# A three-slot weight ring placed at other distances from the activations, in a TensorE-bound decoder kernel

## The reference

```python
def swiglu(h, w_gate, w_up, w_down):
    return (jax.nn.silu(h @ w_gate) * (h @ w_up)) @ w_down

for l in range(DEPTH):                                   # DEPTH = 2
    x = x + 0.5 * swiglu(rms_norm(x, ffn1_norm[l]), ...)  # 1024 -> 2816 -> 1024
    h = rms_norm(x, mix_norm[l])
    pa, pb, pc, pd = jnp.split(h @ w_in[l], IN_SPLITS, axis=-1)
    ...                                                   # four attention mixers
    x = x + jnp.concatenate([ya, yb, yc, yd], axis=-1) @ w_out[l]
    x = x + 0.5 * swiglu(rms_norm(x, ffn2_norm[l]), ...)
    x = rms_norm(x, final_norm[l])
# then one layer of the second kind, with w_in_2 of 1024 x 7424
```

## Time and profile before

| | us |
|---|---|
| median of 2 runs | 1314.11 (1311.85 to 1316.36) |
| the profiled execution | 1319.89 |
| its span, first to last instruction | 1317.6 |
| PE busy | 1265.6 (96%) |
| weight loads busy | 1239.5 (94%) |
| DVE busy | 841.5 (64%) |
| ACT busy | 640.0 (49%) |

### The profile page before, as it was taken

One profiled execution on the slowest core, in us unless ns is written; L12 is line 12 of the kernel. 1 busy time (PEld: TensorE's weight loads), 2 busy tenths in 40 slices (PEclk: granted clock), 3 DMA queues, 4 the chain that ended last, 5 costly groups with the idle time before them and its releaser, 6 DMA issues.

```text
span 1317.6 us, 24755 instructions
## 1 busy us (share of the span) xinstructions
PE 1265.6 (96%) x10500; PEld 1239.5 (94%) x10500; DVE 841.5 (64%) x1059; ACT 640.0 (49%) x850; POOL 78.7 (6%) x57
## 2 busy tenths in 40 slices
PE   6999999988999999999999997999999999999997
PEld 6999999978999999999999996899999989899995
DVE  5766677775676666876667686476666754446665
ACT  4433346754543334533335764453333554766542
POOL 1110011210000000000000211000000000000000
PEclk9999999986999999999999995799999999999999
DMA  8876665320565655566665530256655655415542
GB/s 287 219 227 206 191 224 172 114 87 2 182 200 193 191 191 192 170 199 195 194 219 163 166 132 12 65 165 219 192 191 191 200 178 174 128 58 168 176 152 105
DMA packets 169514, 220.33 MB, mean 167 GB/s; under 512 B 5280, under 2 KB 152480, under 8 KB 169312
## 3 DMA queue, kind: packets, MB, share of 16 engines
q1 hardware_dynamic: 165680, 213.66, 50.8%
q0 software_dynamic: 2080, 2.48, 1.0%
q10 hardware_dynamic: 1680, 3.13, 0.7%
HBM read 218.15 MB, written 3.42 MB: 168 GB/s over the span
## 4 chain that ended last, share of the span: by engine, by line
PE 86%; ACT 6%; DVE 5%; issue 1%; DMA 1%; SPq 0%; POOLq 0%; POOL 0%; DVEq 0%; ACTq 0%
PE pj L433 12%; PE pj L437 12%; PE pj L436 12%; PE acc L437 8%; PE acc L436 8%; PE acc L433 8%; PE tr L433 6%; PE tr L437 6%; PE tr L436 6%; PE acc L616 4%; ACT probs L994 2%; ACT w_hi L875 1%; PE tr L608 1%; DVE w_lo L1186 1%; PE tr L586 1%
## 5 line engine op out<-in xcount | busy, mean ns | idle before, releaser
L1186 DVE TENSOR_TENSOR w_lo<-raw,w_hi 128x2048 fp32r<-128x2048 f32 (+2 forms) x206 | 459.4, 2230 | 241.7 <-ACT w_hi L875 240.3
L875 ACT ACTIVATE w_hi<-raw 128x2048 fp32r<-128x2048 f32 (+2 forms) x206 | 381.2, 1854 | 395.3 <-PE pj L433 142.0
L433 PE MATMUL pj<-hT_hi,w_hi 128*128 128x256 f32 x992 | 277.2, 279 | 3.0 <-DVE w_lo L1186 2.4
L437 PE MATMUL pj<-hT_hi,w_lo 128*128 128x256 f32 x992 | 275.8, 278 | 0.0
L436 PE MATMUL pj<-hT_lo,w_hi 128*128 128x256 f32 x992 | 275.7, 278 | 0.0
L437 PE MATMUL acc<-act_hi,w_lo 128*128 128x256 f32 x704 | 194.3, 276 | 0.0
L433 PE MATMUL acc<-act_hi,w_hi 128*128 128x256 f32 x704 | 194.3, 276 | 0.0
L436 PE MATMUL acc<-act_lo,w_hi 128*128 128x256 f32 x704 | 194.3, 276 | 0.0
L433 PEld LDWEIGHTS pj<-hT_hi,w_hi 128*128 128x128 f32 x992 | 187.5, 189 | 4.5 <-DVE w_lo L1186 2.6
L436 PEld LDWEIGHTS pj<-hT_lo,w_hi 128*128 128x128 f32 x992 | 187.3, 189 | 0.0
L437 PEld LDWEIGHTS pj<-hT_hi,w_lo 128*128 128x128 f32 x992 | 187.1, 189 | 0.0
(11 more groups left out here) (212 smaller groups left out, 1989.6 us busy)
## 6 DMA issues: line engine op xcount, KB each, us to landing
raw<-in_w_in SPq DMA_DIRECT2D x47, 1024.0 KB, 5.3
raw<-in_ffn_w_up SPq DMA_DIRECT2D x44, 1024.0 KB, 5.3
raw<-in_ffn_w_down SPq DMA_DIRECT2D x44, 1024.0 KB, 5.0
raw<-in_ffn_w_gate SPq DMA_DIRECT2D x43, 1024.0 KB, 5.4
raw<-in_w_out SPq DMA_DIRECT2D x12, 1024.0 KB, 4.9
raw<-in_w_proj_a SPq DMA_DIRECT2D x4, 512.0 KB, 3.5
raw<-in_w_proj_b SPq DMA_DIRECT2D x4, 512.0 KB, 3.9
raw<-in_w_proj_c SPq DMA_DIRECT2D x4, 512.0 KB, 3.4
```

The lines of the kernel that those rows point to most:

```text
L433: ins = pe.matmul(out, lhs[0], rhs[0], start=first, stop=False, **kw)
L437: return pe.matmul(out, lhs[1], rhs[0], start=False, stop=last, **kw)
L875: act.activation(w_hi[r % RING][:, 0:w], raw[r % RING][:, 0:w], ACT.Copy).then_inc(hi_set, 1)
L1186: dve.tensor_tensor(w_lo[r % RING][:, 0:w], raw[r % RING][:, 0:w], w_hi[r % RING][:, 0:w].bitcast(F32), ALU.subtract).then_inc(lo_set, 1)
```

## The change

The six tensors `w_hi0..2` and `w_lo0..2` become two, each with three rows of 2048 + 64 elements. A ring slot is a view into a row that starts 60, 4 or 44 elements behind the row's start.

```diff
-        w_hi = [sb(f"w_hi{i}", [P, SLOT], F32R) for i in range(RING)]
-        w_lo = [sb(f"w_lo{i}", [P, SLOT], F32R) for i in range(RING)]
+
+        shift = (60, 4, 44)
+        halves_hi = sb("w_hi", [P, RING, SLOT + 64], F32R)
+        halves_lo = sb("w_lo", [P, RING, SLOT + 64], F32R)
+        w_hi = [halves_hi[:, i, shift[i]:shift[i] + SLOT] for i in range(RING)]
+        w_lo = [halves_lo[:, i, shift[i]:shift[i] + SLOT] for i in range(RING)]
```

## The result

The changed kernel took 1350.88 us (1348.23 to 1353.54, two runs) against 1314.11 us before. The ratio is 1.028 with an interval of 1.0164 to 1.0395, so it is slower for certain, and whether by more than 2% this comparison leaves open. The two medians differ by 37 us, but each rests on two runs. The forecast was 1314 with a range that ended at 1342.

What follows compares the result with a forecast made beforehand. The prediction took PE's matmul rate as the bound. Its terms for instructions, splits and matmuls were all 0, giving 1319.9 + 0 for the profiled execution, or 1314 us for the median; own range 1306 to 1322, stretched to 1284 to 1342.

Steps and rivals of the forecast that it cites:

- Instructions, DMAs and splits: Whole kernel: no instruction or wait changes, DMA target stays put, and the splits L875 and L1186 keep their times; 0 us.
- The bound of a tenth: Splits L875 and L1186: upper bound on their slowdown from shifted starts, a tenth of their mean, 0.19 and 0.22 us.
- Two distances carry the same two rhythms, so the distance has little say: 256-column matmuls: distances +64 and -64 (192 modulo 256) both show 113.3 and about 117.5 ns between starts.
- the term of 0 us for the matmuls: About 9,260 ring-reading matmuls: slots keep their rhythm, loops stay short, mixers' mix is dealt anew; 0, plus or minus 5 us.
- The prediction's own sign of being wrong: Starts within gate, up and down slots: three different rhythms would prove the distance sets the rhythm by itself.
- the prediction's picture of two rhythms that are dealt anew at restarts: Mixer slots: the mix of short (113.3 ns) and long (about 117.5 ns) start spacing is redrawn at restarts; 0 us.
- the border at 185.55: End of a SwiGLU loop before the mixer: said to change the distance yet keep the short rhythm, 113.3 ns.
- The short rhythm is the moving operand's own limit: 256-column matmuls: 113.3 ns lies on the line through 384 and 512 columns, so no distance can beat it.
- the faster rival: 256-column matmuls: a rhythm below 113.3 ns, saving 26 us (1288) or 48 us (1266); chance 0.16.
- The rival that slots fall into the long rhythm: Ring slots turn long as the distance changes at slot borders: 8 us one, 24 all loops, 31 everything (1322 to 1345); 0.30.
- The rival that the change does nothing: Whole kernel: PE never waits for another engine and has two independent read ports, so time stays 1314; no separate chance.
- The small shifts of single starts: 160-column matmuls, whose distance changes per chunk: starts 0.10, 0.12, 0.11 us apart, shifting a few ns with the address.

Runs made afterwards that it cites:

- the kernel with 64 and 144: Kernel before, with ring views by direction: stationary minus moving stays 64 where weights are stationary, becomes 144 where they move; 1313.48 us against 1320.13, ratio 0.9959.

## Why the prediction was wrong

*Instructions, DMAs and splits: right.* Orders and counts are the same, and L1190 and L879 took 2225 and 1852 ns. The bound of a tenth was not needed.

*Two distances carry the same two rhythms, so the distance has little say: wrong, and this is the step that failed.* The reading of the stretch at 196.43 stands: a distance of 192 can carry the short rhythm. What failed is the inference from two distances to all others, and with it the term of 0 us for the matmuls. The three distances that the change brings can't carry it in the loops: their slots went from 113.3 ns to 117.9 at 48, 118.5 at 80 and 117.3 at 240, and 28 us of the loss are in the SwiGLU slots. The prediction's own sign of being wrong was three ring slots with three different rhythms, and it came.

*Nor are 64 and 192 equals.* With stationary weights all slots of the loops hold the short rhythm at 64, and at 192 they run at 117.9 throughout. With moving weights all eleven slots at 64 had it in one run and about three quarters in another, and at 192 only four of 29 in the kernel before. But 192 isn't closed to it either: the run with the gate slot alone entered it there behind a slot at 117.7, and one token-major slot of the kernel before took it up after an interruption of 4 us. These are its second and its last matmul:

```profile
1148.29 0.28 PE L436 MATMUL pj<-w_lo,hT_hi 128*128 128x256 f32 x1
...
1153.50 0.28 PE L437 MATMUL pj<-w_hi,hT_lo 128*128 128x256 f32 x1
```

5.21 us / 46 = 113.3 ns. In the run with shifts of 0, where this slot has the same distance, it ran at 117.8. So at 64 and 192, outside the loops, the prediction's picture of two rhythms that are dealt anew at restarts was right, with the odds depending on distance and direction. I sorted the stretches by what they showed and not by direction, and so took the two distances for equals.

*A misread border.* The prediction says that the border at 185.55 changed the distance and kept the rhythm. The slots on both sides of 185.55 have their weights stationary (`acc<-act_hi,w_hi`); the direction changes at 196.43. There the rhythm did hold, so the argument stands with the other time.

*The short rhythm is the moving operand's own limit: never beaten at 256 columns, but its argument is refuted.* Over 17 distances in either direction nothing with 256 columns came below 113.3 ns, and the faster rival, at 0.16, had no case. The argument was a line through 113.3, 173.3 and 233.3 ns for 256, 384 and 512 columns, and its last point is no limit. These are two starts, 24 matmuls apart, of the 512-column projection in the kernel with 64 and 144:

```profile
1288.94 0.39 PE L441 MATMUL acc<-w_hi,hT_hi 128*128 128x512 f32 x1
...
1294.38 0.39 PE L441 MATMUL acc<-w_hi,hT_hi 128*128 128x512 f32 x1
```

5.44 us / 24 = 226.7 ns, twice 113.3, in three of its four slots, and in one slot of the run with three multiples of 64, where the distance is 0. With 144 everywhere the same four slots took 231 to 232 ns. So 233.3 was a rhythm of one distance, the 192 of the kernel before, and whether 113.3 is a limit at 256 columns isn't shown.

*The rival that slots fall into the long rhythm: right in its direction, a little small, and wrong in its mechanism.* Its price for everything long was 31 us, which ended at 1345; the slots added up to about 34, because the new rhythms are up to 118.6 ns in the loops, and many slots outside that had been at 117.8 moved to 118.3 or 120.0. But the reason given was the change of distance at the slot border. The run with one distance of 48 for all lost at least as much, and the run with the gate slot alone at 48 left its neighbours at 113.3. The odds for it should not have hung on how often rhythms are disturbed, but on how many of the untested distances can be good. At 0.30 it was well below what that deserved.

*The rival that the change does nothing: out.* It took PE to be indifferent to where its two operands lie. Here the instructions, their order and their waits are the same, and the distance between the two operands alone moved the starts from 113.3 to about 118 ns.

*The small shifts of single starts: given too little weight.* They were the one row of before in which the distance did change from chunk to chunk, and starts moved by a few ns. That slot's mean stayed at 111 ns in every run of the study. Continued down to 160 columns, the line above would give 68 ns, so by that estimate the stream has time to spare there, and with 256 columns it has none, so that the same few ns go straight into the sum. That this is the reason is argued and not shown.

## What to carry to other kernels

In this kernel's float32r products of 256 columns, the distance between the addresses of the stationary and the moving operand modulo 256 bytes was worth 3 to 9% of the distance between starts (116.7 to 123.3 ns against 113.3), and the natural allocation sat on the good point by luck. Before a buffer is moved or padded, read the distance of starts within one slot of the timeline, and read it again after. Where several states can hold at one setting, a sample in the good state shows that the setting allows it and not that it brings it about: count how often it does, and sort the samples by direction first. And where a whole family of values is untested, one or two good values say little about their neighbours.

## What the runs showed of the hardware that I had not expected

With stationary weights the good place at 64 is a single element wide: 113.3 ns at 64, 119.4 at 60 and 118.3 at 68 bytes. Several rhythms can exist at one distance (117.8, 118.3 and 123.3 ns at 48), and a loop of 24 slots stays in the one in which it began. What decides which rhythm a stream takes up isn't explained, nor is why 144 is good in one direction only.

At the lower level of the clock (1.2 of 2.4 GHz) the distance cost nothing. In both kernels the first slot of the second layer's output projection starts at that level, behind some 50 us in which PE worked with pauses. The distance is 64 in the kernel before and 48 in the changed one. The stretch (columns as in the earlier trace rows; its clock is 0.50) and two starts of it, before:

```profile
838.20:840.30 2.10, 2.10 (x12) 0.50 0.00 0
```

```profile
838.13 0.41 PE L436 MATMUL acc<-hT_lo,w_hi 128*128 128x256 f32 x1
...
839.41 0.41 PE L436 MATMUL acc<-hT_lo,w_hi 128*128 128x256 f32 x1
```

And in the changed kernel:

```profile
857.00:859.20 2.20, 2.20 (x12) 0.50 0.00 0
```

```profile
856.86 0.41 PE L440 MATMUL acc<-hT_lo,w_hi 128*128 128x256 f32 x1
...
858.14 0.41 PE L440 MATMUL acc<-hT_lo,w_hi 128*128 128x256 f32 x1
```

Both are 1.28 us / 6 = 213.3 ns. That is less than twice 113.3, so the short rhythm isn't a fixed number of clock periods. In the run with three multiples of 64 the same slot, at a distance of 128, has 213 to 214 ns at that level as well.

The same program's profiled executions differ by more than such effects. The kernel with shifts of 0 had the rhythms of the kernel before in all its loops, and these were the two spans and mean granted clocks, first of the kernel before:

```profile
core 0: 1317.6 us, clock 0.968
```

```profile
core 0: 1306.1 us, clock 0.974
```

In the loops both were granted the full clock, and the rows of the loops agree to 0.01 us. The 11.5 us lie in the stretches between. There PE pauses and the clock falls at times to its lower level (1.2 of 2.4 GHz): 1317.6 x 0.032 is 42 us of clock lost, 1306.1 x 0.026 is 34 us. About 2 us more come from slots outside the loops that ran long in one execution and short in the other. So a change of 5 us doesn't show in the difference of two spans, but does in the distance of starts.
